# A paged decoding stage prepared under the projection before it, with a new order of its rounds

## The reference, cut to what matters

```python
h = rmsnorm(x, norm_g) @ w_in
gb, gc, hv, q, k, v, fl = jnp.split(h, splits, axis=-1)
yc, new_hist = causal_dwconv(gc * hv, hist, conv_w)
y_a = gb * yc                                   # gated convolution
q = rmsnorm(q.reshape(bsz, t, N_HEADS_B, HEAD_DIM), q_g)
k = rmsnorm(k.reshape(bsz, t, N_HEADS_B, HEAD_DIM), k_g)
...
k_all = jnp.concatenate([k_pool[page_table].reshape(bsz, p_len, h, d), k_new], axis=1)
v_all = jnp.concatenate([v_pool[page_table].reshape(bsz, p_len, h, d), v_new], axis=1)
s = jnp.einsum('bqhd,bkhd->bhqk', q, k) * HEAD_DIM ** -0.5 + cq - ck
p = jax.nn.softmax(s, axis=-1)
out = jnp.einsum('bhqk,bkhd->bqhd', p, v)
...
y = x + jnp.concatenate([y_a, out], axis=-1) @ w_out
```

## Time and profile before

| | us |
|---|---|
| median of 3 runs | 1616.98 |
| lowest, highest | 1614.31, 1627.02 |
| profiled execution, its own time | 1622.88 |
| its span, first to last instruction | 1621.0 |
| TensorE busy | 1492.5 (92%) |
| VectorE, ScalarE, GpSimd busy | 737.1, 474.0, 593.9 |
| mean granted clock of TensorE | 0.944 |

### The profile page before, as it was taken

The page is one execution under the profiler, slowest core; times in us unless marked ns, Lnnn a source line. Parts: engine busy times, 40 slices in busy tenths (PEclk is TensorE's granted clock), DMA queues, the critical chain, the costliest instruction groups (busy, mean ns, idle before and its releaser), DMA issues.

```text
span 1621.0 us, 39149 instructions
## 1 busy us (share of the span) xinstructions
PE 1492.5 (92%) x16060; PEld 1358.7 (84%) x16060; DVE 737.1 (45%) x1287; ACT 474.0 (29%) x688; POOL 593.9 (37%) x322
## 2 busy tenths in 40 slices
PE   4994898888797999999999999998799999999998
PEld 3993566656566999999999998786699999999998
DVE  5535655656554445440144435676635442034421
ACT  3373122212122332223222233112633432122222
POOL 3221111212113335554454434543125554445531
PEclk9996597988789999999999999999899999999999
DMA  5313575766546323223332244665122322332222
GB/s 166 118 48 111 181 234 179 229 214 214 181 153 191 101 66 100 82 68 93 99 91 81 66 117 118 166 156 139 40 76 81 88 81 83 96 96 86 66 74 77
DMA packets 245222, 190.72 MB, mean 118 GB/s; under 512 B 11992, under 2 KB 204968, under 8 KB 245016
## 3 DMA queue, kind: packets, MB, share of 16 engines
q1 hardware_dynamic: 244188, 186.83, 38.5%
q10 hardware_dynamic: 768, 1.60, 0.3%
q0 software_dynamic: 144, 0.52, 0.1%
HBM read 170.93 MB, written 6.02 MB: 109 GB/s over the span
## 4 chain that ended last, share of the span: by engine, by line
PE 84%; DVE 7%; issue 4%; ACT 3%; DMA 1%; SPq 1%; ACTq 0%; POOL 0%; DVEq 0%; POOLq 0%
PE banks L1678 63%; PE banks L1920 5%; PE banks L1791 4%; PE banks L2059 2%; DVE k_grp L1254 2%; PE banks L1844 2%; PE banks L1872 1%; PE banks L1799 1%; PE banks L1882 1%; PE banks L1893 1%; PE banks L1860 1%; PE banks L1760 0%; PE banks L2011 0%; DMA w_raw<-in_w_out 0%; PE banks L1726 0%
## 5 line engine op out<-in xcount | busy, mean ns | idle before, releaser
L635 POOL TENSOR_TENSOR w_l<-w_raw,w_h 128x1024 fp32r<-128x1024 f32 (+2 forms) x196 | 441.9, 2257 | 440.6 <-ACT w_h L759 419.1
L1678 PE MATMUL banks<-xa_h,w_h 128*128 128x272 f32 x1856 | 388.8, 291 | 8.6 <-DVE x L1093 4.4
L1678 PE MATMUL banks<-xa_h,w_l 128*128 128x272 f32 x1856 | 385.4, 289 | 0.0
L1678 PE MATMUL banks<-xa_l,w_h 128*128 128x272 f32 x1856 | 383.9, 288 | 0.0
L1678 PEld LDWEIGHTS banks<-xa_h,w_h 128*128 128x128 f32 x1856 | 293.9, 189 | 10.7 <-issue 5.1
L1678 PEld LDWEIGHTS banks<-xa_l,w_h 128*128 128x128 f32 x1856 | 293.1, 189 | 0.0
L1678 PEld LDWEIGHTS banks<-xa_h,w_l 128*128 128x128 f32 x1856 | 291.0, 190 | 0.0
L759 ACT ACTIVATE w_h<-w_raw 128x1024 fp32r<-128x1024 f32 (+2 forms) x193 | 185.2, 961 | 201.5 <-PE banks L1678 201.2
L1678 PE MATMUL banks<-h_h,w_h 128*128 128x272 f32 x960 | 201.6, 291 | 9.1 <-DVE h_l L1647 9.0
L1678 PE MATMUL banks<-h_h,w_l 128*128 128x272 f32 x960 | 199.9, 290 | 0.0
L1678 PE MATMUL banks<-h_l,w_h 128*128 128x272 f32 x960 | 199.5, 289 | 0.0
(11 more groups left out here) (282 smaller groups left out, 1817.1 us busy)
## 6 DMA issues: line engine op xcount, KB each, us to landing
w_raw<-in_w_up SPq DMA_DIRECT2D x88, 512.0 KB, 3.7
k_grp<-in_cache_k SPq DMA_DIRECT2D x128, 256.0 KB, 4.1
v_pg<-in_cache_v SPq DMA_DIRECT2D x128, 256.0 KB, 3.8
w_raw<-in_w_in SPq DMA_DIRECT2D x24, 512.0 KB, 5.5
w_raw<-in_w_down SPq DMA_DIRECT2D x32, 384.0 KB, 3.1
w_raw<-in_w_pw SPq DMA_DIRECT2D x24, 512.0 KB, 3.8
w_raw<-in_w_down SPq DMA_DIRECT2D x32, 320.0 KB, 3.1
w_raw<-in_w_out SPq DMA_DIRECT2D x8, 512.0 KB, 4.7
```

Source lines behind the costliest of these rows:

```text
L635: g.tensor_tensor(w_l[:, slot, 0:n], w_raw[:, slot, 0:n], w_h[:, slot, 0:n].bitcast(F32), ALU.subtract).then_inc(s_lo, 1)
L1678: ins = mm(out[:, half, 0:HT], w, v[:, half * HT:(half + 1) * HT], start=first and t == 0 and n == 0, stop=last and t == phase.tiles - 1 a ...
```

## The change

It touches the first projection, the 37 rounds and the hand-over to the output projection:

- the query blocks' memset, the selectors, the query copies and the bias run inside the projection's turns 2, 8 and 9, the first key transpose in turn 10; the clear of the four banks is dropped; TensorE's first scores wait for the last variance (`s_hv`) instead of the last normed head (`s_qk`), which only block scores and later steps wait for;
- VectorE's round begins with the transpose of the next group, and the scaling of gate halves, the taps and the sums stand in another order; the three taps of a channel are spread over rounds;
- TensorE's round has all four value pages behind the scores, and the gate half between `block_value` and `block_score`;
- ScalarE copies the ten row blocks instead of VectorE;
- 21 of the 24 gate halves lie in rounds 2 to 31 (20 in rounds 5 to 31 before), the last three in rounds 32 to 34;
- eight value buffers instead of six, requested one round earlier; two of the four first slabs of the output projection are requested in rounds 31 and 33; one buffer instead of two for turned probabilities (`pt`).

```diff
-KS, VS = 4, 6
+KS, VS = 4, 8
-ROWS_IN = {0: (0, 1, 2, 3), 1: (4, 5, 6), 2: (7, 8, 9)}
+ROWS_IN = {0: (0, 1, 2, 3, 4), 1: (5, 6, 7), 2: (8, 9)}
@@ gate_halves
-    for n in range(4, NROUND):
-        upto = (n - 3) * 20 // (NGRP - 4) if n < NGRP else 20 + (n - NGRP + 1)
+    for n in range(1, NROUND):
+        upto = n * 21 // (NGRP - 1) if n < NGRP else 21 + (n - NGRP + 1)
...
+def conv_pieces(halves_of):
+    end = {q // 2: n for n, qs in halves_of.items() for q in qs if q % 2}
+    out = {}
+    for c in range(4):
+        a, b = end[3 * c + 1], end[3 * c + 2]
+        assert b > a
+        for k in range(CA):
+            out.setdefault(a + k * (b - a) // CA, []).append((c, k))
+    return out
@@ SyncE
+                elif n in (4, 5, 6):
+                    sp.wait_ge(s_kd[n - 4], 32 if n == 4 else 16)
+                elif n == 7:
+                    sp.wait_ge(s_qk, 8)
-                    if n >= LAG - 1 and n - LAG + 1 < NGRP:
-                        value_page(4 * (n - LAG + 1) + j)
+                    if n >= LAG - 2 and n - LAG + 2 < NGRP:
+                        value_page(4 * (n - LAG + 2) + j)
+                    elif q % 2 == 0:
+                        out_load(q // 2 - 10)
-            for j in range(4):
+            for j in range(2, 4):
                 out_load(j)
@@ ScalarE
-                if k >= 2:
-                    act.wait_ge(s_po, k - 1)
-                A(pt[:, k % 2, 0:(w + 1) * P], p_bank[:, 0:(w + 1) * P], ACT.Copy).then_inc(s_ev, 1)
+                if k:
+                    act.wait_ge(s_po, k)
+                A(pt[:, 0:(w + 1) * P], p_bank[:, 0:(w + 1) * P], ACT.Copy).then_inc(s_ev, 1)
+                if n == 9:
+                    q_blocks(0)
+                for r in ROWS_IN.get(n, ()):
+                    rows_read(r)
...
+                for q in halves_of.get(n - 1, ()):
+                    if q % 6 == 5:
+                        gate_high(q // 6)
@@ VectorE, turns of the projection
+                if n == 2:
+                    selectors()
...
+                    V.memset(q_blk[:, :, :, :, :], 0.0).then_inc(s_qb, 1)
+                    after()
...
+                if n == 9:
+                    dve.wait_ge(s_qb, 1)
+                    queries_placed()
+                if n == 10:
+                    key_turned(0)
-            V.memset(raw_scores, 0.0).then_inc(s_clr, 1)
@@ VectorE, a round
+                if more:
+                    key_turned(n + 1)
                 if 1 <= n <= BLOCKS:
                     block_inverse(n - 1)
                 if n < NGRP:
                     logits(n)
-                if more:
-                    key_turned(n + 1)
+                if p == 0 and 1 <= b <= NB:
+                    biggest(b - 1)
+                if p == 3 and n < NGRP:
+                    new_logits(b)
...
+                for q in halves_of.get(n, ()):
+                    half_scaled(q)
...
+                for c, k in pieces.get(n, ()):
+                    conv_tap(c, k)
@@ TensorE
-            pe.wait_ge(s_qk, 8)
+            pe.wait_ge(s_hv, 8)
-            pe.wait_ge(s_clr, 1)
...
                 if values_at >= 0:
-                    value_page(values_at)
-                    value_page(values_at + 1)
+                    for j in range(4):
+                        value_page(values_at + j)
...
+                if n < NGRP:
+                    keys_back(n)
...
+                if 2 <= n < BLOCKS + 2:
+                    block_value(n - 2)
+                for q in halves_of.get(n, ()):
+                    gate_half(q, n)
                 if p == 0 and 1 <= b <= NB:
                     max_spread(b - 1)
+                if n == 0:
+                    pe.wait_ge(s_qk, 8)
                 if n < BLOCKS:
                     block_score(n)
```

More of the change, by code:

```diff
@@ L799, in head_root, with q_blocks @@
                 A(tmp[:, c % 2, :], tmp[:, c % 2, :], ACT.Exp, scale=-0.5).then_inc(s_hrt, 1)
+            def q_blocks(half):
+                act.wait_ge(s_qb, 1)
+                for part in range(2):
+                    for i in range(4):
+                        at = 2 * half + part
+                        A(q_blk[32 * i:32 * i + 32, :, at, :, NT * half:NT * half + NT],
+                          qkv[32 * at:32 * at + 32, 0:4, TP:T].rearrange("p c (b t) -> p c b t", t=NT), ACT.Copy).then_inc(s_qb, 1)
             for n in range(12):
@@ L876, in gate_high, with rows_read @@
                 A(h_h[:, c, :], ug[:, :], ACT.Copy).then_inc(s_hhi, 1)
[L878 to L884, removed]
-                          qkv[32 * at:32 * at + 32, 0:4, TP:T].rearrange("p c (b t) -> p c b t", t=NT), ACT.Copy).then_inc(s_qb, 1)
             gate_split(0)
             gate_split(1)
-            act.wait_ge(s_qk, 8)
-            q_blocks(0)
+            def rows_read(r):
+                t, kv = r % 5, 1 - r // 5
+                act.wait_ge(s_rows, r + 1)
+                if r == 5 + 3:
+                    act.wait_ge(s_kd[0], 16)
+                n = P if t < 4 else TS
+                dst = s_row[:, kv, :] if t == 4 else v_tok[:, t, :] if kv else k_row[t % 3][:, :]
+                A(dst, bank[r % 2][0:n, :], ACT.Copy).then_inc(s_rowsd, 1)
             for n in range(NROUND):
@@ L1319, in placed, with half_scaled @@
                  .then_inc(s_owr, 1)
[L1321 to L1331 removed]
+            def half_scaled(q):
                 g, half = q // 2, q % 2
@@ L1335, in gate_out @@
                 if q == 0:
-                    for n in range(3):
-                        dve.wait_ge(s_kd[n], 32 if n == 0 else 16)
+                    dve.wait_ge(s_rows, 5)
                 dst = uh if t else uc
@@ L1392, in _ @@
                     logits(n)
-                if more:
-                    key_turned(n + 1)
+                if p == 0 and 1 <= b <= NB:
+                    biggest(b - 1)
+                if p == 3 and n < NGRP:
+                    new_logits(b)
                 if p == 1 and b >= 2:
                     placed(b - 2)
-                for r in ROWS_IN.get(n, ()):
-                    rows_read(r)
+                if p == 2 and 1 <= b <= NB:
+                    inverse(b - 1)
+                for q in halves_of.get(n, ()):
+                    half_scaled(q)
+                if p == 0 and 1 <= b <= NB:
+                    shift(b - 1)
+                if n < BLOCKS:
+                    bias(n)
+                if p == 0 and 1 <= b <= NB:
+                    total(b - 1)
+                for q in halves_of.get(n, ()):
+                    gate_out(q)
+                for c, k in pieces.get(n, ()):
+                    conv_tap(c, k)
+                for q in halves_of.get(n - 1, ()):
+                    if q % 6 == 5:
+                        gate_low(q // 6)
                 if n == 2:
```

150 lines of the change are left out of this document (59 added, 91 removed).

## The result

The changed kernel takes 1624.27 us (median of 11 runs, 1619.7 to 1630.54); the kernel before, on the same chip, takes 1614.08 (median of 11, one of them a slow one of 2373.3 us that the ratio leaves out). The ratio is 1.006, 95% interval 1.0034 to 1.0087. The forecast was 1562 with a range of 1538 to 1594. It missed by 62 us and had the wrong sign.

What follows compares the result with a forecast made beforehand. TensorE's waits and slow clock before 526 us were taken as what the change could move. Start 9.2 + rounds 5 to 31 40.5 + last five rounds 11.1 = 60.8 us off 1622.88 gave 1562, range 1538 to 1594.

Steps and rivals of the forecast that it cites:

- Start: Up to round 5: preparation moved under the projection, scores near 133 instead of 145.5, round 5 near 186; 9.2 us won.
- the rule that the prediction set beside its estimate: Query copies: GpSimd shares SBUF interfaces with VectorE, so with GpSimd idle the copies cost 1.4 us, otherwise 4.6.
- 226 + 11 + 8 + 12 = 257: Rounds 5 to 31: work, wait for old sums, VectorE's loop, slow clock; 257 against 297.5 us, 40.5 won.
- 12.8 us of issue at the value matmuls: Rounds 5 to 31: taken for late value pages, mostly won by requesting them about two rounds ahead.
- the wait for the old sums: Rounds 5 to 31: once per batch value matmuls wait for VectorE to scale old sums; 1.60 us x 7 = 11.
- Clock: Rounds 5 to 31: half the former share at 1.2 GHz, 15% of the time at some 1.6 times the duration, 12 us.
- Key transposes: Rounds 5 to 31: 8.1 us of waits in front of the scores; with the transpose first, it is never late.
- Tail: Last five rounds and hand-over: 7.86 us wait goes, one gate half already done; 33.3 to 22.2, 11.1 us won.
- become the loop: Rounds 5 to 31: VectorE's chain sets the pace, rounds with a half take 10 us; 278 us, total 1583; chance 0.18.
- Rival 3: Rounds: nothing gained, transpose waits reappear at the logits; start and tail alone give 20 us or 10 to 15; 1610; chance 0.08.
- Rival 4: Rounds 5 to 31: TensorE stays at 1.2 GHz, 14 us a round, 81 us lost, 20 won; 1684; chance 0.05.
- Rival 2: Rounds 5 to 31: page transfers bind; at 199 GB/s 11.4 us a round, no gain there, 1603; chance 0.05.

Runs made afterwards that it cites:

- b4_start: Kernel before with only the paged stage's preparation (queries placed, selectors, first key transpose, TensorE's first waits) moved into the first projection; 1609.21 us, ratio 0.9956.
- b3_split: Changed kernel with TensorE's four value pages split again, two behind the score group and two at the round's end; 1596.63 us, ratio 0.9877 to the kernel before.
- c4_keylast: b3_split with VectorE's key transpose put back behind the logits of its round; 1604.07 us, ratio 0.9928 to the kernel before.
- a4_nopages: Changed kernel with only the first 8 of the 128 value pages loaded, so part of the computation is changed; 1602.04 us, ratio 0.9948 to the kernel before.
- b1: a2 with 128 instructions (waits already met) added ahead of TensorE's first transposes; 1608.11 us, ratio 0.9946 to the kernel before.
- a2: Changed kernel with VectorE's reading of a finished batch's values moved from the next round into the turn round; 1608.31 us, ratio 0.9972 to the kernel before.
- e1: Changed kernel with value pages 0 and 1 behind the score group, 2 and 3 in mid-round behind keys_back; 1615.89 us, ratio 1.0008 to the kernel before.
- e2: Changed kernel with all four value pages in a row at the round's end; 1607.90 us, ratio 0.9938 to the kernel before.
- b2_pad64: a2 with 64 instructions (waits already met) added ahead of TensorE's first transposes; 1603.70 us, ratio 0.9916 to the kernel before.

## Why the prediction was wrong

**Start: right.** The scores begin at 132.75 (133 forecast), the second group at 144.48 (145.8), round 5 at 182.9 (186): 12.3 us won, 9.2 forecast. Alone, in b4_start, half of it reaches the end. The 16 query copies, now at 120.7 to 124.1 us with GpSimd idle, take 165 to 179 and 215 to 223 ns each, as the rule that the prediction set beside its estimate had it; the copy of 2286 ns is gone.

**Rounds 5 to 31: wrong, and here it failed.** The step was "226 + 11 + 8 + 12 = 257". The clock record and the busy times give 51.9 us idle and 257.5 busy, 92 of them at 1.2 GHz (81 of 257.3 before). An estimate: if work takes twice as long there, the lower level adds 46 us to 211.5 of work; at the 1.7 times of a gate half it adds 38 to 219.6. So the work was 6 to 14 us less than I took, the clock 26 to 34 more, idle 33 more (19 forecast). The step had no term for stops of TensorE by its own program, counted the issue time as won and halved the slow clock on the strength of that.

*Idle.* I read 12.8 us of issue at the value matmuls as late pages, and counted it won by an earlier request. They ended at no engine, but at no DMA either, and the stop fell inside a group of 16 records of one kind:

```profile
266.88 0.49 PE L1844 MATMUL banks<-v_pg,pr 128*8 128x128 f32 x9
271.67 0.61 PE L1844 MATMUL banks<-v_pg,pr 128*8 128x128 f32 x7 [4.29 <-issue]
```

Its fetch ran from 269.46 to 270.45. Such stops went from 17.7 to 31.0 us over the stage, 28.3 of them in rounds 5 to 31. The second item, the wait for the old sums, I took at 1.6 x 7 = 11 us; it was 9.9 in the rounds, about as taken, and 7.7 behind them.

*Clock.* I took half of the former share because idle time would mostly go (15% of the time at 1.6 times the duration is nearer 13 us than my 12). It did not go: 296.20:299.60 above stands at 0.50 behind a stop, and the clock falls at 378.1, 398.6 and 429.3 us, 0.7 to 1.2 us behind the ends of stops of 2.19, 2.62 and 2.88 us (377.12, 397.89, 428.06). The stage has 22 falls against 15 before (13 in b3_split). Of the 21 times that TensorE stood for 1.2 us or more, whatever it waited for, 17 have a fall during them or within 2.5 us of their end, and the slow stretch lasts 3.4 to 17 us. So most such stops are paid twice, as idle time and as work at half clock behind it.

**Key transposes: right.** 8.1 to 0.8 us of waits, 8 us of time by c4_keylast. **Tail: wrong.** The last wait went from 7.86 to 2.19 us, but 35.2 us took the place of 22.2: a wait of 7.70 us came in at round 33, behind VectorE's chain. I had named that chain for the rounds and forgot it in round 33. TensorE is busy for 24.1 us and not 20.2 (23.4 less a gate half), at a clock of 0.77 and not 0.91.

**Rivals.** None names what happened. VectorE did not become the loop (167 of 309 us), and TensorE never waited for pages over 0.2 us. Rival 3 has the nearest time, for other reasons. Rival 4 had the sign, but the clock stood at 0.84, no lower level all through. Rival 2's "only if pages come in bursts" was half of it: the transfers don't hold up the pages' readers but the fetch of the program behind them (without 120 of them, 18 us less in a4_nopages). Against that rival's cap, 152 to 162 us after the change shows 374 GB/s, more than the 321 I had seen and than the 358 that I had set beside it; the measurement decides.

**Open.** That stops end with the fetch of the program is shown; that they account for the whole difference is not, since b1 has the most issue time and is faster than a2. Why pages at the round's end shorten the stretches at the lower clock more than pages behind the score group isn't settled; e1 and e2 only say where they have to stand.

## What to carry to other kernels

Idle time that the profile calls issue, inside a run of equal instructions that wait for nothing, can be the fetch of the program: look whether an instruction packet landed just before it ended, and try orders that put slower work ahead of dense stretches of tiny instructions (b3_split gave 1.8%). Price a stop of a microsecond or more as idle time plus the slow clock behind it. When a wait is moved off the end, follow the engine that was waited for some rounds back, for the chain may only have changed its place.

## What was not expected of the hardware

- TensorE's program comes in 16 KB packets on a queue of its own, on the DMA engines that carry the pages; after a stop TensorE goes on 1.2 to 1.8 us after one has landed. With these engines 98% busy the packet of 293.72 started 4.1 us after TensorE had passed the place 256 instructions ahead of the stop (289.64); with them idle, that of 297.03 started 1.1 us after it had passed the stop itself (295.91).
- 64 instructions that do nothing, 12 us into the program, moved the time by 0.56% (a2_values to b2_pad64, intervals of 0.2%, on two chips). Differences of that size between two orders of a fully unrolled stage can come from where its pieces end.
- Waits that are already met are not free: in b1_pad128 TensorE's 128 added instructions run from 5.56 to 19.36 us, 107 ns each. The first 64 hide in its idle time (b2_pad64: first transpose at 12.63 us, not 12.21), the others move it to 19.47.
